# A two-layer decoder trunk on one core: ScalarE reads the last tile from PSUM, the last root lies in PSUM, and GpSimd adds three blocks to the residual

## The chip, the cores and the metric

The kernel runs on one core of one Trainium2 chip. The metric is the device time of one execution in microseconds (us), as a median over runs. Beside the timed runs there is one execution taken by the hardware profiler; it gives the rows shown here.

## The reference

Two layers are applied to 512 prompt tokens and 8 decode tokens that share one set of weights. Cut to what matters here:

```
h = x + RMSNorm_post ( Mixer ( RMSNorm_pre (x) ) )
y = h + RMSNorm_post2( SwiGLU( RMSNorm_pre2(h) ) )

RMSNorm(f, w) = f * rsqrt(mean(f*f) + eps) * w          # over the 1024 features of a token
SwiGLU(h)     = (silu(h @ Wgate) * (h @ Wup)) @ Wdown    # 22 blocks of 128 hidden features
```

Mixer is a gated DeltaNet group and a retention group between an input and an output projection; the change doesn't touch it. The change is in the last line of the last layer: the down projection gives f, the sum of squares over its features gives the root, and f, weighted by w and multiplied by the root, is added to the residual h.

## The kernel before, in words

**Layout.** Activations lie transposed: features on the 128 partitions in KT = 8 blocks, tokens in the free dimension. The 520 tokens are split in two halves `a` = 0 and 1 of HC = 260 columns each. `hT[:, k, a]` is block k of the residual in half a, `fT[:, k, a]` the same block of the sublayer's output; both are fp32 in SBUF. One block of one half is 128 x 260 x 4 bytes = 133,120 bytes.

**The down projection.** TensorE makes the eight output blocks one after the other. Each is a sum over 22 hidden blocks, with three matmuls per hidden block and half (values are split in a high and a low part). Blocks 0 to 6 are done for both halves together. The last block, k = 7, is made half by half: all 66 matmuls of half 0 into PSUM bank 2 (semaphore `half_done`), then those of half 1 into bank 3 (`tile_done`). The matmuls that add up squares over the partitions (`sum_added` at L692, `norm_sum` at L698) are put into that second run: after hidden block 0 and hidden block 2 of half 1 for half 0; after the last one for half 1. They write banks 4 and 5.

**The norm.** For each block, VectorE copies PSUM to `fT`, ScalarE squares it into `sqb` (`square`, L1333) and then weights `fT` in place by the norm's weight (`weigh`, L1382). `root_mean` is two ScalarE instructions: Ln from PSUM (L1344) and Exp (L1345), which leave the root in `rb[:, a]` in SBUF. `new_h` is run by VectorE for a group of blocks k0 to k1: it multiplies `fT` by the root (L1908), waits for that, and adds the product to `hT` (L1909). Each semaphore wait stands in the in-order queue of its engine: what is behind it waits too.

**The end of the last layer.** VectorE copies block 7 of half 0 (L2577), runs `new_h` for half 0 in the groups (0,1), (1,2), (2,3), (3,4), (4,6), (6,8), and, between the last two of them, copies block 7 of half 1 from PSUM (L2589). Then it runs `new_h` for half 1 in the three groups of `LAST`. SyncE sends five parts of `hT` to `yT` (L566), each when `h_ready` has reached its last block; the last three parts are the groups of `LAST`:

```
LAST = [(0, 4), (4, 7), (7, 8)]
Y_PARTS = [(0, 0, 4), (0, 4, 8)] + [(1, k0, k1) for k0, k1 in LAST]
```

**GpSimd** has other work earlier in the kernel (decay factors, some products, and the loads and stores of the decode states); nothing of it is in the last stage after its last store.

Of the kernel before, what the change touches and what calls it, by code (L numbers as in the profile page):

```python
# [8 lines left out]
def trunk(nc, xT, w_slabs, w_ba, w_rows, dt_bias, a_log, conv_hist, state_gdn, state_ret, c_f32, c_rope,  # L9
# [4 lines left out]
    ALU = mybir.AluOpType  # L14
    ACT = mybir.ActivationFunctionType

    P = 128
# [82 lines left out]
    with ctx:  # L100
# [285 lines left out]
        def heads_of(i):  # L386
# [1 line left out]
            return i // 2, slice((i % 2) * P, (i % 2 + 1) * P)  # L388

        names = (  # L390
            "const_loaded mask_loaded row_loaded early_loaded adt_loaded rope_reloaded x0_loaded x1_loaded x2_loaded "
            "x3_loaded x4_loaded first_loaded slab0_loaded slab1_loaded dst0_loaded dst1_loaded dst0_stored dst1_stored tail_stored "
            "state_stored y_stored a_stored a_loaded xq_stored x_loaded "

# [78 lines left out]
        block = ctx.enter_context(nc.Block())  # L473


        LAST = [(0, 4), (4, 7), (7, 8)]
        Y_PARTS = [(0, 0, 4), (0, 4, 8)] + [(1, k0, k1) for k0, k1 in LAST]

        @block.sync
        def _(sp):  # L480
# [37 lines left out]
            sp.dma_start(cf[:], c_f32).then_inc(s["const_loaded"], 16)  # L518
            sp.dma_start(wba[:], w_ba).then_inc(s["early_loaded"], 16)
            sp.dma_start(rope[:], c_rope).then_inc(s["early_loaded"], 16)  # L520
            sp.dma_start(mask[:], c_mask).then_inc(s["mask_loaded"], 16)
            sp.dma_start(histT[:], conv_hist).then_inc(s["early_loaded"], 16)
            for l in range(DEPTH):
                for n in range(SLABS):
# [49 lines left out]
        def _(pool):  # L574
# [13 lines left out]
            for l in range(DEPTH):  # L588
                def read_state(u):
                    if u < 2:  # L590

                        for a in range(2):
                            pool.wait_ge(s[f"tile_free{a}"], l * TILES // 2 + 4)
                    else:
                        pool.wait_ge(s["dr_mm"], l * 16 + u - 1)
                    load_state(l, u, True)

                def masked_step(i):
                    if i == 0:
                        pool.wait_ge(s["mask_loaded"], 16)  # L600
                        pool.wait_ge(s["xq_stored"], (l + 1) * 32)
                    mk = mask[:, 0:1, :].unsqueeze(1).to_broadcast([P, 2, 2, P])
                    to = T[:, i].rearrange("p (c a) n -> p c a n", c=2)
                    nc.gpsimd.tensor_tensor(to, MT[:, 2 * i:2 * i + 2, 2:4], mk, ALU.mult).then_inc(s["mtk_ready"], 1)

                def keys_decayed(c):
                    if c == 0:
                        pool.wait_ge(s["mt_ready"], (l + 1) * NC)
                        pool.wait_ge(s["kt_ready"], (l + 1) * NC)
                    nc.gpsimd.tensor_tensor(ktok[:, c], ktok[:, c], over_cols(c2[:, c, :]), ALU.mult).then_inc(s["kd_ready"], 1)  # L610

                def decay_rests(c):
                    if c >= 2:
                        pool.wait_ge(s["dec_mm"], l * NC + c - 1)
                    else:
                        pool.wait_ge(s["g_split"], l + 1)
                        pool.wait_ge(s["rod_mm"], (l + 1) * NC)
                        pool.wait_ge(s["state_stored"], l * 32)
                    nc.gpsimd.tensor_tensor(dinl[c % 2], over_heads(m_le), over_cols(g2[:, 1, c].bitcast(fp32)), ALU.mult).then_inc(s["dkl_ready"], 1)

                for u in range(8):
                    read_state(u)
                for c in range(NC):
                    decay_rests(c)
                for u in range(8, 10):
                    read_state(u)
                for c in range(NC):

                    pool.wait_ge(s["a_ready"], l * NC + c + 1)
                    nc.gpsimd.tensor_tensor(MT[:, c, 2:4], MT[:, c, 2:4], Ab[:, 0:2, c], ALU.add).then_inc(s["cm_ready"], 1)  # L630
                pool.wait_ge(s["aT_T"], (l + 1) * NC)
                nc.gpsimd.memset(kqpad, 0.0).then_inc(s["x_zeroed"], 1)
                pool.wait_ge(s["cm_ready"], (l + 1) * NC)
                pool.wait_ge(s["a_stored"], (l + 1) * NBK * 16)
                nc.gpsimd.memset(Xc[:].rearrange("p i h c n -> p (i h c n)"), 0.0).then_inc(s["x_zeroed"], 1)
                pool.wait_ge(s["tO_T"], (l + 1) * NC)
                nc.gpsimd.memset(XT[:].rearrange("p c h n -> p (c h n)"), 0.0).then_inc(s["x_zeroed"], 1)
                masked_step(0)
                masked_step(1)
                for u in range(10, 16):  # L640
                    read_state(u)
                for c in range(NC):
                    keys_decayed(c)
                for c in range(1, NC):
                    pool.wait_ge(s["qs_mm"], l * (NC - 1) + c)
                    pool.wait_ge(s["s_ready"], l * NC + c)
                    nc.gpsimd.tensor_tensor(S[:], S[:], over_cols(egc[:, 1, c, :]), ALU.mult).then_inc(s["s_decayed"], 1)
                pool.wait_ge(s["dr_mm"], (l + 1) * 16)
                pool.wait_ge(s["w_rest"], l * REST + (Q - 1) * W_STEPS + W_LO05)
                load_state(l, 0, False)  # L650
                load_state(l, 1, False)
                for u in range(16):
                    store_state(l, u)
                    if u < 14:
                        pool.wait_ge(s[f"dst{u % 2}_stored"], 16 * (l * 8 + u // 2 + 1))
                        load_state(l, u + 2, False)
                if l + 1 < DEPTH:
                    for a in range(2):
                        pool.wait_ge(s[f"dst{a}_stored"], 16 * (l + 1) * 8)
                    pool.dma_start(rope[:], c_rope).then_inc(s["rope_reloaded"], 16)  # L660

        @block.tensor
        def _(pe):
# [624 lines left out]
        def _(act):  # L1288
# [16 lines left out]
            for l in range(DEPTH):  # L1305
# [26 lines left out]
                    to = sqh[:, k % 2] if a is None else sqh[:, k % 2, a]  # L1332
                    A(to, src, ACT.Square).then_inc(s["sq_ready" if n % 2 else "xsq_ready"], 2 if a is None else 1)  # L1333

                def root_mean(n, a, l=l):
                    T0 = l * TILES
                    if n % 2 == 0:
                        act.wait_ge(s["x_sums"], nth_norm(l, n) + nth(l, n, KT - 1, a))
                    else:
                        act.wait_ge(s["norm_sum"], (l * 2 + n // 2) * 2 + a + 1)  # L1340

                        for u in range(2):
                            act.wait_ge(s[f"tile_free{u}"], (T0 + (32 if n == 1 else T_DN)) // 2)
                    step(A(rb[:, a], PS[:, 4 + a, 0:HC], ACT.Ln, scale=1.0 / D, bias=EPS))  # L1344
                    A(rb[:, a], rb[:, a], ACT.Exp, scale=-0.5).then_inc(s["rb_ready"], 1)  # L1345

                def round_x(n, k, a, l=l):

# [142 lines left out]
                for t in range(32):  # L1491
# [4 lines left out]
                    if t == 6:  # L1496
                        act.wait_ge(s["gate_pre"], l + 1)
                        if l == 0:
                            act.wait_ge(s["adt_loaded"], DEPTH * 32)
                        A(gb[:], ga[:, :, 0:H], ACT.Exp, scale=-1.0)  # L1500
                        A(adt[:, l, 1, :], adt[:, l, 1, :], ACT.Exp)
                        step(A(gs[:], gs[:], ACT.Exp, scale=-1.0))
# [309 lines left out]
                def square_down(k):  # L1812
# [3 lines left out]
                    else:  # L1816
                        square(3, k, fT[:, k, 1], 1)

                for i in range(KT * FT // 8 - NW):
                    hi(G0 + S_DN + i + NW)  # L1820
                    for k in range(KT - 2):
# [3 lines left out]
                                weigh(3, k - 1, fT[:, k - 1])  # L1825
                weigh(3, KT - 3, fT[:, KT - 3])
                square_down(KT - 2)
                act.wait_ge(s["half_free"], (l + 1) * SPLIT)
                square(3, KT - 1, fT[:, KT - 1, 0], 0)
                weigh(3, KT - 2, fT[:, KT - 2])  # L1830
                weigh(3, KT - 1, fT[:, KT - 1, 0], 0)
                if l + 1 < DEPTH:
                    root_mean(3, 0)
                    hi(G0 + SLABS)
# [17 lines left out]
                    second_x(0, l + 1)  # L1852
                else:
                    root_mean(3, 0)
                    square_down(KT - 1)
                    weigh(3, KT - 1, fT[:, KT - 1, 1], 1)
                    root_mean(3, 1)

        @block.vector
        def _(dve):  # L1860
# [12 lines left out]
            for l in range(DEPTH):  # L1873
# [201 lines left out]
                for t in range(32):  # L2075
# [39 lines left out]
                    if t == 5:  # L2115
# [2 lines left out]
                        step.go(V.tensor_copy(places, flat2(rD[:, 0:H]).rearrange("p (u j) -> p j u", j=4)))  # L2118
                        dve.wait_ge(s["bad_done"], l + 1)
                        if l == 0:  # L2120
                            dve.wait_ge(s["adt_loaded"], DEPTH * 32)
                        step.go(V.tensor_copy(ga[:, 0:NC, :].rearrange("p c h -> p (c h)"), PS[:, 7, B_BA:B_BA + NC * 2 * H]))
                        step(V.tensor_copy(ga[:, NC:NG, :].rearrange("p c h -> p (c h)"), PS[:, 6, 0:NB * 2 * H]))
                        step(V.tensor_tensor(ga[:, :, H:2 * H], ga[:, :, H:2 * H], adt[:, l, 0, :].unsqueeze(1).to_broadcast([P, NG, H]), ALU.add))
# [448 lines left out]
                    if 3 <= i < 19:  # L2573
                        new_state(i - 3)
                down_tile(KT - 2)
                dve.wait_ge(s["half_done"], (l + 1) * SPLIT)
                V.tensor_copy(fT[:, KT - 1, 0], PS[:, 2, 0:HC]).then_inc(s["half_free"], 1)  # L2577
                dve.wait_ge(s["half_free"], (l + 1) * SPLIT)
                for k0, k1 in (*TOGETHER[:2], (2, 3), (3, 4), *TOGETHER[3:]):
                    new_h(3, k0, k1, 0)  # L2580
                    if k0 == 0:
# [1 line left out]
                    for k in range(max(k0 - 1, 0), k1 - 1 if l + 1 < DEPTH else 0):  # L2583
                        rest_x(0, k, 0, l + 1)
                        if k == 1:
                            lo(G0 + SLABS + 1)
                    if k0 == (2 if l + 1 < DEPTH else 4):
                        done(T_DN + KT - 1)
                        freed(V.tensor_copy(fT[:, KT - 1, 1], PS[:, 3, 0:HC]), T_DN + KT - 1)  # L2589
                if l + 1 < DEPTH:  # L2590
                    rest_x(0, KT - 1, 0, l + 1)
                evacuated(T_DN + KT - 1)
                if l + 1 < DEPTH:
                    second_half_x(3, l + 1)
                    lo(G0 + SLABS + 2)
                else:
                    for k0, k1 in LAST:
                        new_h(3, k0, k1, 1)


def _constants(nc_, heads, seq, nb, past_len=4096, rope_base=10000.0):
# [120 lines left out]
```

## Time and profile before

| what | value |
|---|---|
| time, median of 3 runs | 1384.03 us |
| lowest and highest of these | 1383.95 and 1384.6 us |
| the profiled execution's own time | 1382.82 us |
| its span (first to last recorded instruction) | 1381.0 us |
| granted TensorE clock, mean | 0.997 |
| busy share: TensorE, VectorE, ScalarE, GpSimd | 99%, 75%, 46%, 7% |
| HBM read and written | 132.79 and 12.78 MB |

The span is 1.82 us shorter than the profiled execution's own time; that rest lies around the recorded instructions. Times within the trace count from the start of the span. A row of a timeline shows when an instruction starts and how long it takes; in square brackets stands how long its engine had been idle and what released it. In the chain that ended last, each piece is what the next one waited for.

### The profile page before, as it was taken

To read this page: it belongs to the slowest core of one execution; us is meant where nothing else is said; L and a number is where in the kernel's file an instruction comes from. 1 tells how busy PE (TensorE), PEld (TensorE's weight loads), DVE (VectorE), ACT (ScalarE), POOL (GpSimd) and SP (SyncE) were. 2 spreads that over 40 slices of the span, in tenths; PEclk is the share of its full clock that TensorE was granted. 3 is DMA by queue.
4 is the path that set the end of the run, shared out by engine and by line. 5 is a ranking of instruction groups with operands and counts; after the bars stand their busy time and mean duration, and the time that the engine had idled before them with its cause. 6 is when DMAs were issued, how large, how long until landed. Compare 5 with 4: busy or idle time off the path is not lost.

```text
span 1381.0 us, 29088 instructions
## 1 busy us (share of the span) xinstructions
PE 1361.7 (99%) x12172; PEld 1339.7 (97%) x12172; DVE 1039.5 (75%) x1675; ACT 634.9 (46%) x1230; POOL 100.6 (7%) x141
## 2 busy tenths in 40 slices
PE   9999999999999999999999999999999999999997
PEld 8999999999999999999989999999999999999996
DVE  7746896867998898754586558958789989886545
ACT  5235554557544455422442364545575445454221
POOL 0001211000000000011000012110000000000110
PEclk9999999999999999999999999999999999999998
DMA  5322233122323232345413313321222323233542
GB/s 210 112 103 77 73 116 113 32 68 92 104 98 117 96 111 104 121 164 182 131 62 112 115 55 95 108 94 40 75 92 93 123 92 114 101 108 123 174 177 93
DMA packets 67491, 147.46 MB, mean 107 GB/s; under 512 B 20128, under 2 KB 23584, under 8 KB 67360
## 3 DMA queue, kind: packets, MB, share of 16 engines
q1 hardware_dynamic: 59248, 119.37, 25.9%
q0 software_dynamic: 7824, 25.70, 5.3%
q8 instruction: 96, 1.57, 0.5%
q10 hardware_dynamic: 288, 0.52, 0.1%
q14 instruction: 35, 0.29, 0.1%
HBM read 132.79 MB, written 12.78 MB: 105 GB/s over the span
## 4 chain that ended last, share of the span: by engine, by line
PE 88%; DVE 8%; ACT 1%; issue 1%; DMA 1%; SPq 0%; DVEq 0%; ACTq 0%
PE PS L669 48%; PE PS L1224 8%; PE PS L1225 8%; PE PS L1226 8%; PE PS L675 5%; DVE Wl L1871 1%; DVE hT L1909 1%; DVE Xl L1888 1%; DVE mT L1908 1%; PE PS L863 1%; DVE conv L1998 1%; PE PS L1190 1%; PE PS L847 1%; PE PS L835 1%; PE PS L1009 1%
## 5 line engine op out<-in xcount | busy, mean ns | idle before, releaser
L1303 ACT ACTIVATE Wh<-stage 128x1024 fp32r<-128x1024 f32 x143 | 151.1, 1058 | 327.2 <-PE PS L669 300.1
L669 PE MATMUL PS<-Xh,Wh 128*128 128x260 f32 x1376 | 285.3, 288 | 2.3 <-DVE Wl L1933 1.6
L669 PE MATMUL PS<-Xh,Wl 128*128 128x260 f32 x1376 | 277.0, 283 | 0.0
L669 PE MATMUL PS<-Xl,Wh 128*128 128x260 f32 x1376 | 276.5, 282 | 0.0
L1871 DVE TENSOR_TENSOR Wl<-stage,Wh 128x1024 fp32r<-128x1024 f32 x143 | 174.6, 1222 | 105.4 <-ACT Wh L1303 104.6
L669 PEld LDWEIGHTS PS<-Xh,Wh 128*128 128x128 f32 x1376 | 211.4, 189 | 5.6 <-DVE Wl L1933 2.0
L669 PEld LDWEIGHTS PS<-Xh,Wl 128*128 128x128 f32 x1376 | 211.8, 188 | 0.0
L669 PEld LDWEIGHTS PS<-Xl,Wh 128*128 128x128 f32 x1376 | 211.7, 188 | 0.0
L1224 PE MATMUL PS<-XU,hiA 128*128 128x260 f32 x448 | 126.8, 283 | 0.0
L1224 PE MATMUL PS<-XU,hiB 128*128 128x260 f32 x448 | 126.8, 283 | 0.0
L1225 PE MATMUL PS<-XU,hiB 128*128 128x260 f32 x448 | 126.6, 283 | 0.0
L1225 PE MATMUL PS<-XU,hiA 128*128 128x260 f32 x448 | 126.6, 283 | 0.0
L1226 PE MATMUL PS<-XU,loB 128*128 128x260 f32 x448 | 126.4, 282 | 0.0
L1226 PE MATMUL PS<-XU,loA 128*128 128x260 f32 x448 | 126.4, 282 | 0.0
L669 PE MATMUL PS<-actH,Wh 128*128 128x260 f32 x616 | 124.1, 282 | 0.0
L669 PE MATMUL PS<-actH,Wl 128*128 128x260 f32 x616 | 123.9, 282 | 0.0
L669 PE MATMUL PS<-actL,Wh 128*128 128x260 f32 x616 | 123.9, 282 | 0.0
L669 PEld LDWEIGHTS PS<-actH,Wh 128*128 128x128 f32 x616 | 97.2, 188 | 1.4
L669 PEld LDWEIGHTS PS<-actL,Wh 128*128 128x128 f32 x616 | 94.8, 188 | 0.0
L669 PEld LDWEIGHTS PS<-actH,Wl 128*128 128x128 f32 x616 | 94.8, 188 | 0.0
L1225 PEld LDWEIGHTS PS<-XU,hiA 128*128 128x128 f32 x448 | 84.7, 189 | 0.0
L1225 PEld LDWEIGHTS PS<-XU,hiB 128*128 128x128 f32 x448 | 84.7, 189 | 0.0
(384 smaller groups left out, 2865.7 us busy)
## 6 DMA issues: line engine op xcount, KB each, us to landing
stage<-w_slabs SPq DMA_DIRECT2D x143, 512.0 KB, 3.3
raw<-w_slabs SPq DMA_DIRECT2D x136, 256.0 KB, 2.7
dst<-state_ret POOLq DMA_DIRECT2D x32, 256.0 KB, 3.3
dst<-state_gdn POOLq DMA_DIRECT2D x32, 256.0 KB, 3.9
out_gdn_sample<-dst POOLq DMA_DIRECT2D x16, 256.0 KB, 2.9
out_ret_sample<-dst POOLq DMA_DIRECT2D x16, 256.0 KB, 3.2
hT<-x_t SPq DMA_DIRECT2D x3, 520.0 KB, 6.5
out_y_t<-hT SPq DMA_DIRECT2D x3, 520.0 KB, 3.1
```

The costliest lines, as they stand in the source:

```text
L669: ins = mm(pj(slot)[:, a], w[:, ws, pos, :], x[:, a, :], start=first and w is Wh and x is xh, stop=last and w is Wl)
L675: ins = mm(pj(slot)[:, a], w[:, ws, pos, :], x[:, a, :], start=first and w is Wh and x is xh, stop=last and w is Wl)
L835: ins = mm(PS[:, 6, h * P:(h + 1) * P], rT[:, H + h, cs], rT[:, h, cs], start=True, stop=True)
L847: ins = mm(PS[:, 4, h * P:(h + 1) * P], T[:, 0, h, :], T[:, 1, h, :], start=True, stop=True)
L863: ins = mm(PS[rows, 7, B_U:B_U + P], vectors, dst[:, u % 2, j, :], start=n == 0, stop=n == 7 and u < 8, skip_group_check=True)
L1009: ins = mm(PS[:, 4 + c, h * P:(h + 1) * P], kT[:, h, cs], qT[:, h, cs], start=True, stop=True)
L1190: mm(PS[:, 4 + u % 2, :], krows[:, u // 8, :], vblks[u % 2].rearrange("p a n -> p (a n)"), start=True, stop=True).then_inc(s["outer_mm"], 1)
L1224: mm(PS[:, bank, 0:HC], hi_[:, u, cols], XU[:, u, 0, k], start=k == 0 and u in (UA11, US2, US1, UA22), stop=False, skip_group_check=True)
L1225: mm(PS[:, bank, 0:HC], hi_[:, u, cols], XU[:, u, 1, k], start=False, stop=False, skip_group_check=True)
L1226: ins = mm(PS[:, bank, 0:HC], lo_[:, u, cols], XU[:, u, 0, k], start=False, stop=k == 3, skip_group_check=True)
L1303: A(Wh[:, G % NW], stage[:, G % NS], ACT.Copy).then_inc(s["hi_split"], 1)
L1871: V.tensor_tensor(Wl[:, G % NW], stage[:, G % NS], Wh[:, G % NW].bitcast(fp32), ALU.subtract).then_inc(s["lo_split"], 1)
```

## The change

In the last layer only:

- VectorE's two copies of block 7 out of PSUM are gone. A new ScalarE helper, `last_half(a)`, squares the block straight from PSUM and writes the weighted block from PSUM to `fT`. The weighting of block 6 now stands ahead of it.
- The Exp that ends `root_mean` for half 1 writes to PSUM bank 6 instead of `rb[:, 1]`.
- Half 1's residual: VectorE multiplies blocks 0 to 2 by the root, then blocks 3 to 7 (`f_scaled` counts both). GpSimd waits for the first, adds blocks 0 to 2 to `hT`, and raises `h_ready` by 3. VectorE waits for its own two products and for GpSimd's add (by `h_ready`), and then adds blocks 3 to 6 and block 7.
- `LAST` is (0,3), (3,7), (7,8), so the last three stores have other sizes.
- The mask's load near the kernel's start counts on `adt_loaded` instead of a semaphore of its own, whose place `f_scaled` takes; the three waits on `adt_loaded` and the one on the mask wait for all five loads.

```
-        LAST = [(0, 4), (4, 7), (7, 8)]
+        LAST = [(0, 3), (3, 7), (7, 8)]
 ...
-            sp.dma_start(mask[:], c_mask).then_inc(s["mask_loaded"], 16)
+            sp.dma_start(mask[:], c_mask).then_inc(s["adt_loaded"], 16)
 ...
-                        pool.wait_ge(s["mask_loaded"], 16)
+                        pool.wait_ge(s["adt_loaded"], (2 * DEPTH + 1) * 16)
 ...
+            k1 = LAST[0][1]
+            pool.wait_ge(s["f_scaled"], 1)
+            nc.gpsimd.tensor_tensor(hT[:, 0:k1, 1], hT[:, 0:k1, 1], fT[:, 0:k1, 1], ALU.add).then_inc(s["h_ready"], k1)
 ...
-                    A(rb[:, a], rb[:, a], ACT.Exp, scale=-0.5).then_inc(s["rb_ready"], 1)
+                    A(rb[:, a] if root is None else root, rb[:, a], ACT.Exp, scale=-0.5).then_inc(s["rb_ready"], 1)
 ...
+                def last_half(a):
+
+                    if a:
+                        act.wait_ge(s["tile_done"], T0 + TILES)
+                    else:
+                        act.wait_ge(s["half_done"], (l + 1) * SPLIT)
+                    square(3, KT - 1, PS[:, 2 + a, 0:HC], a)
+                    row = R_FPOST + KT - 1
+                    A(fT[:, KT - 1, a], PS[:, 2 + a, 0:HC], ACT.Copy, scale=prm[:, l, row:row + 1]).then_inc(s["f_ready"], 1)
 ...
+                if l + 1 == DEPTH:
+                    weigh(3, KT - 2, fT[:, KT - 2])
+                    last_half(0)
+                else:
                     (the four lines of before)
 ...
                     root_mean(3, 0)
-                    square_down(KT - 1)
-                    weigh(3, KT - 1, fT[:, KT - 1, 1], 1)
-                    root_mean(3, 1)
+                    last_half(1)
+                    root_mean(3, 1, root=PS[:, 6, 0:HC])
 ...
-                    if k0 == (2 if l + 1 < DEPTH else 4):
+                    if k0 == 2 and l + 1 < DEPTH:
                         done(T_DN + KT - 1)
                         freed(V.tensor_copy(fT[:, KT - 1, 1], PS[:, 3, 0:HC]), T_DN + KT - 1)
 ...
-                    for k0, k1 in LAST:
-                        new_h(3, k0, k1, 1)
+                    dve.wait_ge(s["rb_ready"], (l * 4 + 4) * 2)
+                    dve.wait_ge(s["f_ready"], (l + 1) * HN)
+                    for k0, k1 in (LAST[0], (LAST[1][0], KT)):
+                        src = fT[:, k0:k1, 1]
+                        V.tensor_tensor(src, src, PS[:, 6:7, 0:HC].to_broadcast([P, k1 - k0, HC]), ALU.mult).then_inc(s["f_scaled"], 1)
+                    dve.wait_ge(s["f_scaled"], 2)
+                    dve.wait_ge(s["h_ready"], nth_norm(l, 3) + KT + LAST[0][1])
+                    for k0, k1 in LAST[1:]:
+                        V.tensor_tensor(hT[:, k0:k1, 1], hT[:, k0:k1, 1], fT[:, k0:k1, 1], ALU.add).then_inc(s["h_ready"], k1 - k0)
```

## Rows read from the trace of the kernel before

**Rows 1.** The page: span, and the shares of the chain that ended last.

```profile
span 1381.0 us, 29088 instructions
...
PE 88%; DVE 8%; ACT 1%; issue 1%; DMA 1%; SPq 0%; DVEq 0%; ACTq 0%
```

**Rows 2.** Chain that ended last, 1369 to 1381 us: start, length (us), what.

```profile
1368.92 1.09 PE PS L675 x9
...
1370.10 0.44 DVE fT L2589
...
1370.56 0.43 ACT sqb L1333
...
1371.04 0.72 PE PS L698 x2
...
1371.78 0.40 ACT rb L1344
...
1372.20 0.43 ACT rb L1345
...
1372.82 1.25 DVE fT L1908
...
1374.16 1.25 DVE hT L1909
...
1375.44 0.98 DVE fT L1908
...
1376.52 0.98 DVE hT L1909
...
1377.52 0.44 DVE fT L1908
...
1377.98 0.43 DVE hT L1909
```

**Rows 3.** Timeline of half 0's norm and around the last copy: start, us, instruction.

```profile
1361.78 0.42 ACT L1333 ACTIVATE sqb<-fT 128x260 f32<-128x260 f32 x1 [5.76 <-DVE fT L2577]
...
1362.57 0.38 PE L698 MATMUL PS<-sqb,cf 128*128 128x260 f32 x1
...
1369.83 0.60 PE L692 MATMUL PS<-ss,cf 128*128 128x260 f32 x2
...
1371.02 0.51 ACT L1382 ACTIVATE fT<-fT,prm 128x260 f32<-128x260 f32 x1
...
1371.24 0.70 DVE L1909 TENSOR_TENSOR hT<-hT,fT 128x520 f32<-128x520 f32 x1
```

**Rows 4.** Quarter-microsecond windows: busy times, then TensorE clock, DMA share, GB/s.

```profile
1376.25:1376.50 0.25, 0.00 (x0) 0.00 (x0) 0.16 (x1) 0.00 (x0) 0.00 (x0) 0.50 0.53 187
...
1377.75:1378.00 0.25, 0.00 (x0) 0.00 (x0) 0.22 (x2) 0.00 (x0) 0.00 (x0) 0.50 0.53 175
...
1378.25:1378.50 0.25, 0.00 (x0) 0.00 (x0) 0.17 (x1) 0.00 (x0) 0.00 (x0) 0.50 0.19 71
...
1379.75:1380.00 0.25, 0.00 (x0) 0.00 (x0) 0.00 (x0) 0.00 (x0) 0.00 (x0) 0.50 0.81 283
```

**Rows 5.** Groups by line and shape: ScalarE's squares of 260 columns from PSUM.

```profile
L1743 ACT ACTIVATE sqb<-PS 128x260 f32<-128x260 f32 x34 | 12.6, 370 | 0.2
```

**Rows 6.** Timelines of GpSimd and VectorE where both work: 151 to 153, 222 to 227 us.

```profile
152.02 0.73 POOL L630 TENSOR_TENSOR MT<-MT,Ab 128x256 f32<-128x256 f32 x1 [3.52 <-DVE Ab L2025]
...
151.25 0.68 DVE L2025 TENSOR_TENSOR Ab<-PS,brk 128x512 f32<-128x512 f32 x1
...
222.41 4.03 POOL L610 TENSOR_TENSOR ktok<-ktok,c 128x512 f32<-128x512 f32 x4
...
222.53 0.69 DVE L2051 TENSOR_TENSOR T<-PS,brkm 128x512 f32<-128x512 f32 x1 [1.86 <-PE PS L956]
223.14 3.36 DVE L2171 TENSOR_TENSOR sqd<-qkvD 128x32 f32<-128x32 f32 x1
226.42 0.18 DVE L2172 TENSOR_TENSOR sqd<-qkvD 128x32 f32<-128x32 f32 x1
```

**Rows 7.** One line's instructions: count, shortest, median and longest in ns.

```profile
L604 POOL TENSOR_TENSOR T<-MT,mask x4: 1347/1648/1777, 198.4 to 885.3; 128x512 f32<-128x512 f32 x4
```

More of the change, by code:

```diff
@@ L390, in trunk @@
         names = (
-            "const_loaded mask_loaded row_loaded early_loaded adt_loaded rope_reloaded x0_loaded x1_loaded x2_loaded "
+            "const_loaded f_scaled row_loaded early_loaded adt_loaded rope_reloaded x0_loaded x1_loaded x2_loaded "
             "x3_loaded x4_loaded first_loaded slab0_loaded slab1_loaded dst0_loaded dst1_loaded dst0_stored dst1_stored tail_stored "
@@ L1333, in square, with root_mean @@
                     A(to, src, ACT.Square).then_inc(s["sq_ready" if n % 2 else "xsq_ready"], 2 if a is None else 1)
-                def root_mean(n, a, l=l):
+                def root_mean(n, a, l=l, root=None):
                     T0 = l * TILES
@@ L1498, in _ @@
                         if l == 0:
-                            act.wait_ge(s["adt_loaded"], DEPTH * 32)
+                            act.wait_ge(s["adt_loaded"], (2 * DEPTH + 1) * 16)
                         A(gb[:], ga[:, :, 0:H], ACT.Exp, scale=-1.0)
@@ L1827, in _ @@
                 square_down(KT - 2)
[L1828 to L1831, printed above, removed]
+                if l + 1 == DEPTH:
+                    weigh(3, KT - 2, fT[:, KT - 2])
+                    last_half(0)
+                else:
+                    act.wait_ge(s["half_free"], (l + 1) * SPLIT)
+                    square(3, KT - 1, fT[:, KT - 1, 0], 0)
+                    weigh(3, KT - 2, fT[:, KT - 2])
+                    weigh(3, KT - 1, fT[:, KT - 1, 0], 0)
                 if l + 1 < DEPTH:
@@ L2120, in _ @@
                         if l == 0:
-                            dve.wait_ge(s["adt_loaded"], DEPTH * 32)
+                            dve.wait_ge(s["adt_loaded"], (2 * DEPTH + 1) * 16)
                         step.go(V.tensor_copy(ga[:, 0:NC, :].rearrange("p c h -> p (c h)"), PS[:, 7, B_BA:B_BA + NC * 2 * H]))
@@ L2575, in _ @@
                 down_tile(KT - 2)
-                dve.wait_ge(s["half_done"], (l + 1) * SPLIT)
-                V.tensor_copy(fT[:, KT - 1, 0], PS[:, 2, 0:HC]).then_inc(s["half_free"], 1)
-                dve.wait_ge(s["half_free"], (l + 1) * SPLIT)
+                if l + 1 < DEPTH:
+                    dve.wait_ge(s["half_done"], (l + 1) * SPLIT)
+                    V.tensor_copy(fT[:, KT - 1, 0], PS[:, 2, 0:HC]).then_inc(s["half_free"], 1)
+                    dve.wait_ge(s["half_free"], (l + 1) * SPLIT)
                 for k0, k1 in (*TOGETHER[:2], (2, 3), (3, 4), *TOGETHER[3:]):
@@ L2591, in _ @@
                     rest_x(0, KT - 1, 0, l + 1)
-                evacuated(T_DN + KT - 1)
+                    evacuated(T_DN + KT - 1)
                 if l + 1 < DEPTH:
```

## The prediction

> **What bounds the kernel now.** I read the page first. TensorE carries 88% of the chain that ended last and VectorE 8% [rows 1]. The edits to the computation lie after or beside the last matmuls of layer 2, so what they are worth is read there, not from the shares. Next the same chain, narrowed to the last microseconds [rows 2]. The reader is to see one serial tail. The last matmul ends at 1368.92 + 1.09 = 1370.01. Then come the copy of block 7 (VectorE), its square (ScalarE), the sum over partitions (TensorE), Ln and Exp (ScalarE), and from 1372.82 six VectorE instructions, a product and a sum for each group of `LAST`, to 1378.41. Nothing overlaps in it.
>
> Third, the timeline around it, for what lies beside the chain [rows 3], and last the stores in windows of a quarter microsecond [rows 4]. The DMA engines are busy in two solid stretches. The first begins about 1376.37 (0.53 of the window that ends at 1376.50) and ends at 1377.88: 1.51 us for the four blocks that were ready at 1375.40. The second begins at 1378.45 and ends at 1379.95, 1.50 us for the three blocks ready at 1377.50 and the one ready at 1378.41. So a store's bytes begin to move 0.97 us after the sum (1376.37 - 1375.40; 0.95 in the other case), and a block takes 1.51 / 4 = 0.38 us (133,120 bytes at some 350 GB/s). The last block alone could have begun at 1378.41 + 0.97 = 1379.38, but the three ahead of it are through only at 1378.45 + 3 x 0.38 = 1379.59. The end is therefore set by the store of the second group, not by the last sum: already before, the last block queues for 0.2 us.
>
> **The change part by part.**
>
> *The start.* The mask's load changes its semaphore. All five loads lie in the first stage, and the first reader of the mask runs near 198 us [rows 7]. Nothing is added; cost 0. Were a load late after all, GpSimd, VectorE and ScalarE would each wait in order behind it, but 100 us and more of other work covers it.
>
> *Half 0.* Without the copy, the square can start about 0.45 us before 1361.78. But its sum stands in TensorE's queue after hidden block 2 of half 1, at 1362.57, behind a square that had ended at 1362.20 [rows 3]. TensorE did not wait for it, so worth 0; its cover is 0.37 us. Moving the weighting of block 6 ahead costs nothing, because ScalarE had been idle 5.76 us there [rows 3]. VectorE, which no longer copies block 7 of half 1, finishes half 0 near 1370.85 instead of 1371.94 [rows 3]; it then waits for the root anyway. Worth 0 too.
>
> *Block 7 of half 1 from PSUM.* The copy goes. Before, 0.55 us passed from the matmul's end to the square (1370.01 to 1370.56, [rows 2]); a wake-up of 0.07 remains, so ScalarE starts at 1370.08. The square from PSUM costs 0.37 [rows 5] against 0.42: TensorE's sum starts at 1370.08 + 0.43 = 1370.51. TensorE is free then: its first part of the sum starts 1369.83, lasts 0.60 and ends at 1370.43 [rows 3]. That is a cover of only 0.08 us. With 0.72 for the sum and 0.02 to ScalarE, Ln starts at 1371.25, Exp 0.42 later at 1371.67, and VectorE 0.62 after that, all steps as in [rows 2]: 1372.29 instead of 1372.82. Gain 0.53. The weighting, 0.51 before [rows 3], runs beside the sum in either kernel. Where Exp writes is priced as before: no row has an Exp into PSUM. Above, I bound it by the present 0.42; below, by a read of PSUM, 0.37, so 0.05 either way.
>
> *Products.* A VectorE operation of 260, 780, 1040 columns takes 0.43, 0.98, 1.25 (chain, [rows 2]): 0.27 per block on 0.16. The product over three blocks ends at 1372.29 + 0.98 = 1373.27. That over five costs 0.16 + 5 x 0.27 = 1.51 and ends at about 1374.80. Its PSUM operand should not make it dearer: 512 columns with one operand in PSUM took 0.69 [rows 6], where this scale gives 0.16 + 512/260 x 0.27 = 0.69.
>
> *GpSimd's sum.* It starts 0.09 us after VectorE's signal (151.25 + 0.68 = 151.93 to 152.02, [rows 6]), at 1373.36. No row has 780 columns. The nearest, two full fp32 operands of 256 columns, is 0.73 [rows 6]. In proportion that gives 0.73 x 780/256 = 2.22, the upper bound if GpSimd has any fixed cost. The lower comes from 4.03/4 = 1.01 per 512 columns with a small second operand [rows 6]: 1.54. The dearest row, 1.78 for 512 columns of bf16 mask beside VectorE work [rows 7], gives 2.71 and stays as an outer bound. I take 2.0, near the first row, less a small fixed part. GpSimd ends at 1375.36. VectorE, finished at 1374.80, waits for it; both remaining sums and both last stores are queued behind that wait. With 0.1 to wake it (my estimate, as in the other direction), it adds four blocks from 1375.46 to 1376.70 and block 7 to 1377.16. Before: 1378.41. So the arithmetic ends 1.25 us sooner.
>
> The case turns on whether the product and GpSimd's sum run together. At 222.41 four GpSimd operations fill 4.03 us. A VectorE operation with one PSUM operand started at 222.53 and took its usual 0.69; the next, both operands from SBUF and only 32 columns, took 3.36, until GpSimd was through, against 0.18 for its like [rows 6]. The products now read the root from PSUM, so they are of the first kind; the sums are of the second, but they start after GpSimd. The Trainium skill says the same (SBUF — State Buffer, "Who interferes with whom": a VectorE instruction with at most one SBUF input, outside the two-port modes, does not contend with GpSimd, one with two does against a GpSimd read); the trace agrees, 0.69 against 3.36. A second rule speaks against the change: the Trainium skill (GPSIMD Engine Reference, "Elementwise — side-by-side cycle accounting") gives 4497 ns on GpSimd for a 2048-column fp32 add against 2293 on VectorE. In proportion, an estimate of 1.71 us for 780 columns: slower than VectorE's 0.98, yet shorter than my 2.0, and by it the gain would be 0.3 more.
>
> *Stores.* Here most of the 1.25 goes. GpSimd's three blocks: bytes from 1375.36 + 0.97 = 1376.33 to 1377.46. The four blocks ready at 1376.70: from 1377.67 for 1.51 to 1379.18. The last, ready at 1377.16, could flow at 1378.13 but queues until 1379.18 and ends at 1379.56, against 1379.95. The last store now queues for one microsecond, since its predecessor has four blocks instead of three.
>
> *Sum.* 0.39, say 0.4 us less: on the profiled execution 1382.82 (span 1381.0 and 1.82 around it) becomes 1382.4, and on the median, which is 1.21 higher, 1384.03 becomes 1383.6.
>
> **The rivals.**
> - *All of the arithmetic's gain reaches the end.* If stores overlap rather than queue, the end follows the last sum: 1384.03 - 1.25 = 1382.8. A GpSimd sum of 1.5 us comes near it: then the four-block sum starts at 1375.0, gain 0.9. Against it: four blocks took the same 1.5 us as one store or as two [rows 4].
> - *GpSimd is dearer than thought (slower than before).* Each 0.1 us of its sum moves the four-block store by 0.1. Break-even is 2.0 + 0.4 = 2.4 us; with 2.71 [rows 7] the kernel ends 0.3 later: 1384.3. For it: the row exists. Against: that row had VectorE operations on two SBUF operands beside it, and another type.
> - *The two engines exclude each other after all.* GpSimd starts after the second product, at 1374.89, and ends at 1376.89; four blocks are summed by 1378.23, and bytes end at 1378.23 + 0.97 + 1.89 = 1381.09, 1.14 later: 1385.2. The 0.69 in [rows 6] speaks against it.
> - *Something elsewhere moves*, by a shifted instruction stream in the 1370 us that are unchanged. Nothing in the profile speaks for it.
>
> **How the numbers follow.** A measurement of this kernel can tell about 0.2% from no change, 2.8 us, twice what the whole tail could give. Chances: forecast (gain 0.1 to 0.8, 1383.2 to 1383.9) 0.55; all of the gain or near it, 0.18; dear GpSimd 0.15; exclusion 0.05; something elsewhere 0.07, of which 0.03 beyond 0.2% faster and 0.02 slower. The first four all lie within 0.2%, so same is 0.95. The range takes in the first rival (1382.8) and the second (1384.3), each with 0.3 for the scatter that the three runs show: 1382.5 to 1384.6.
>
> **What the profile after should show.** The square of block 7 starts 0.1 us after the last matmul. VectorE's first product of half 1 starts 2.3 us after it instead of 2.8. GpSimd's one operation lasts about 2.0 us, beside an undisturbed 1.5 us product. VectorE idles some 0.7 us, released by GpSimd, then two sums. DMA is busy without a gap for 1.9 us at the end, starting about 1.0 us after the four-block sum. The prediction would be wrong if the five-block product is stretched, if GpSimd takes over 2.4 us, or if a span outside the last 11 us moves.

## The result: 0.18% slower, and the profile after

The changed kernel takes 1386.15 us (median of 21 runs, 1384.53 to 1389.37) against 1383.95 us for the kernel before (21 runs, 1382.14 to 1385.27): ratio 1.0018, 95% interval [1.0012, 1.0024]. The forecast was 1383.6 us, within 1382.5 to 1384.6; it missed on the slow side by 2.55 us. The ratio lies just under the 0.2% that the prediction gave as the least that can be told, but the interval does not hold 1: by it the change costs 1.7 to 3.3 us.

I count a **tail** from the end of half 1's last matmul to the end of the span, since the point where the tail begins moves by itself: it lay between 1369.8 and 1372.5 in the fourteen profiled executions of this case, with no order by kernel. Two things in the part that the change leaves alone go with it. In six traces (the changed kernel, three variants of it and two of the kernel before) TensorE pauses for 1.1 to 1.3 us near 208 us, waiting for ScalarE's `bv`, and the last matmul ends at 1371.5 to 1372.5. In three others the granted TensorE clock was 0.83 instead of 1.00 between 5 and 15 us, and it ends at 1371.1 to 1371.5. The five with neither end at 1369.8 to 1370.8. Why an execution has the one or the other was not tried. Before, the tail is 1381.0 - 1370.01 = 10.99 us. In the changed kernel the span is 1385.8 and the last matmul ends at 1372.16, so the tail is 13.64: 2.65 longer. The chain that ended last in the changed kernel (start, length, what):

```profile
1367.97 4.19 PE PS L678 x35
1372.16 0.44 PE PS L695 x2
1372.60 0.04 issue
1372.64 0.72 PE PS L701 x2
...
1373.38 0.40 ACT rb L1347
...
1373.80 0.40 ACT PS L1348
...
1374.23 0.41 issue
1374.65 0.98 DVE fT L2618
...
1375.73 1.87 POOLq L100
...
1377.72 1.24 DVE hT L2622
1378.97 0.34 DVEq L100
```

and its groups of instructions in the last 14 us (x count, busy us, mean ns, idle before and its releaser):

```profile
L663 POOL TENSOR_TENSOR hT<-hT,fT 128x780 f32<-128x780 f32 x1 | 1.8, 1829 | 18.1 <-DVE fT L2618 18.1
L2618 DVE TENSOR_TENSOR fT<-fT,PS 128x1300 f32<-128x1300 f32 x1 | 1.5, 1501 | 0.0
L2622 DVE TENSOR_TENSOR hT<-hT,fT 128x1040 f32<-128x1040 f32 x1 | 1.2, 1242 | 0.7 <-POOL hT L663 0.7
...
L1336 ACT ACTIVATE sqb<-PS 128x260 f32<-128x260 f32 x1 | 0.4, 387 | 6.0 <-PE PS L678 6.0
```

The chain names the GpSimd sum by L100, since the exit's instruction already stands in GpSimd's queue, and it stops at VectorE's last sum: stores and exit are not in it. Up to there the end of the work is as forecast, though not each step. VectorE's first product starts 2.49 us after the last matmul (forecast 2.28, before 2.81). GpSimd's sum took 1.83 us, VectorE waited 0.7 us for it, and the last sum ended at 1377.72 + 1.58 = 1379.30. That is 7.14 us after the last matmul; forecast 7.15, before 8.40. The stores, in the same quarter-microsecond windows as [rows 4]:

```profile
1378.50:1378.75 0.25, 0.00 (x0) 0.00 (x0) 0.25 (x1) 0.00 (x0) 0.00 (x0) 0.50 0.82 287
...
1379.75:1380.00 0.25, 0.00 (x0) 0.00 (x0) 0.00 (x0) 0.00 (x0) 0.00 (x0) 0.50 0.23 83
...
1381.75:1382.00 0.25, 0.00 (x0) 0.00 (x0) 0.00 (x0) 0.00 (x0) 0.00 (x0) 0.50 0.35 113
1382.00:1382.25 0.25, 0.00 (x0) 0.00 (x0) 0.00 (x0) 0.00 (x0) 0.00 (x0) 0.50 0.00 0
```

The last byte moves at 1381.84, 9.68 us after the last matmul, against 9.94 before. But then nothing is busy for 3.96 us, where 1.05 passed before (1379.95 to 1381.0). The instructions of the program's exit say why (all have one line; op, duration ns, first and last start). First the changed kernel, then the kernel before:

```profile
L100 POOLq EVENT_SEMAPHORE  x2: 17/17/17, 1385.7 to 1385.7; - x2
...
L100 POOLq DRAIN  x1: 9876/9876/9876, 1375.7 to 1375.7; - x1
...
L100 SPq DRAIN  x1: 7/7/7, 1382.6 to 1382.6; - x1
...
L100 SPq EVENT_SEMAPHORE  x1: 17/17/17, 1385.8 to 1385.8; - x1
```

```profile
L100 POOLq DRAIN  x1: 8564/8564/8564, 1355.0 to 1355.0; - x1
...
L100 SPq DRAIN  x1: 7/7/7, 1380.8 to 1380.8; - x1
```

Every engine ends with a drain, and then they meet. SyncE is through at 1382.6 and waits for GpSimd. GpSimd's drain stands in its queue from 1375.73 and takes 9.88 us: 1.87 us of it is the sum itself (the chain's piece), 8.01 us comes after the sum. The drain is not new. In the kernel before it follows GpSimd's last store at 1355.0 and takes 8.56 us, of which some 0.55 is that issue: 8.0 us again, but over at 1363.5, and nobody notices.

### The profile page after: what moved, and what is told of

Same layout as the page of the kernel before. It is cut to its first block, busy times and chain, and to the rows that moved or that the text cites. A ratio compares the mean times of both kernels' runs of the same rounds, so it can differ in the third digit from the quotient of the medians.

```text
span 1385.8 us, 29080 instructions
## 1 busy us (share of the span) xinstructions
PE 1362.8 (98%) x12172; PEld 1340.0 (97%) x12172; DVE 1039.4 (75%) x1671; ACT 634.6 (46%) x1230; POOL 103.0 (7%) x142
## 4 chain that ended last, share of the span: by engine, by line
PE 87%; DVE 8%; ACT 1%; issue 1%; DMA 1%; SPq 0%; POOLq 0%; DVEq 0%; ACTq 0%
PE PS L672 48%; PE PS L1227 8%; PE PS L1228 8%; PE PS L1229 8%; PE PS L678 5%; DVE Wl L1887 1%; DVE hT L1925 1%; DVE Xl L1904 1%; DVE mT L1924 1%; PE PS L866 1%; DVE conv L2014 1%; PE PS L1193 1%; PE PS L850 1%; PE PS L838 1%; PE PS L1012 1%
```

## The experiments

All runs stand beside runs of the kernel before on the same chip. "The drain beyond its instruction" is the closing GpSimd drain less the part in which its last instruction still runs.

### VectorE does GpSimd's sum

```
-            pool.wait_ge(s["f_scaled"], 1)
-            nc.gpsimd.tensor_tensor(hT[:, 0:k1, 1], ..., ALU.add)
...
-                    dve.wait_ge(s["h_ready"], nth_norm(l, 3) + KT + LAST[0][1])
-                    for k0, k1 in LAST[1:]:
+                    for k0, k1 in LAST:
```

> The changed kernel without its GpSimd sum: VectorE adds blocks 0 to 2 itself, then 3 to 6 and 7; all else as changed. I count the tail from the end of half 1's last matmul to the span's end: 10.99 us before (1370.01 to 1381.0), 13.64 after (1372.16 to 1385.8). Theory (closing drain): in the changed kernel GpSimd's drain ends about 8.0 us after its last instruction, and the program waits for it. Without that instruction the drain starts after GpSimd's last store, near 1357, and is hidden: the tail is set by the stores again, about 2.49 to the first product + 2.4 for two products + 0.1 + 2.5 for three sums = 7.5, stores done at about 10.0, end at 11.0; time 1384.0, as before. Rival A (the loss is in the new store sizes or in the longer wait of the last store): the sizes are the same, so the tail stays above 13 and the time near 1386.2. Rival B (something earlier in the program was shifted by the new semaphore use): unchanged here too, 1386 or so, with a last matmul near 1372.

Measured 1384.1 us (11 runs; before 1383.75; ratio 1.0002 [0.9993, 1.001]). The last matmul ended at 1371.42 and the span at 1382.5, a tail of 11.1. GpSimd's exit:

```profile
L100 POOLq DRAIN  x1: 8564/8564/8564, 1356.4 to 1356.4; - x1
```

The loss is gone with the one GpSimd instruction and the wait for it, though the sizes of the stores, the PSUM reads and the semaphores are those of the changed kernel. Rivals A and B fall.

### The PSUM reads alone

```
-                    square_down(KT - 1)
-                    weigh(3, KT - 1, fT[:, KT - 1, 1], 1)
+                    last_half(1)
                     root_mean(3, 1)
```
(and the same for half 0; `LAST` and `new_h` as before, root in SBUF)

> The kernel before with one part of the change alone (and the mask's semaphore as changed): ScalarE squares and weights block 7 from PSUM, VectorE's two copies are gone. The root stays in SBUF, the three groups are (0,4), (4,7), (7,8), VectorE does all sums. By my prediction's own term for this part the tail shrinks by 0.53 from 10.99 to 10.5 and the time is 1383.5. Rival A: reading PSUM from ScalarE twice costs what the copy did, tail 11.0, time 1384.0. Rival B (something earlier is shifted by the mask's new semaphore): 1385.5 with a tail of 10.5.

1383.69 us (11 runs; before 1383.75; ratio 0.9998 [0.9989, 1.0007]); last matmul 1370.00, span 1380.7, tail 10.70. The chain:

```profile
1370.47 0.72 PE PS L698 x2
...
1371.63 0.43 ACT rb L1345
1372.06 0.04 DVEq L1918
1372.10 0.41 issue
1372.51 1.25 DVE fT L1921
```

The sum over partitions starts 0.57 us earlier than in [rows 2]; TensorE is no obstacle. But between Exp and the first product 0.45 us pass instead of 0.20, so 0.30 of the forecast 0.53 remains. All ten profiled kernels without VectorE's copy have the pause of about 0.4 before this product, whether Exp writes to SBUF or PSUM; the four with the copy have not. It isn't a matter of a long wait alone: in half 0 of the kernel before, VectorE had waited 2.39 us and started 0.09 after Exp. Its cause wasn't tried.

### A fill that nobody waits for, at three times

The kernel before, with one more GpSimd instruction; the three differ in its wait:

```
+            pool.wait_ge(s["h_ready"], DEPTH * 2 * HN - 4)
+            nc.gpsimd.memset(gs[:], 0.0)
```

After half 1's first sum:

> The kernel before with one more GpSimd instruction: a fill of 48 columns of a buffer that nobody reads any more, after VectorE's first sum of half 1. Nobody waits for it. Theory (closing drain of 8.0 us after GpSimd's last instruction, and the program ends only after it): VectorE's first sum ends 5.39 us after the last matmul, so 5.39 + 0.1 + 0.1 + 8.0 + 0.2 = 13.8 instead of 10.99, and the time is 1384.0 + 2.8 = 1386.8. Rival (the changed kernel lost because of what its GpSimd sum does or what waits for it, or by stores): nothing waits here and nothing is stored, so 1384.0 and a tail of 11.0.

After the last sum (`DEPTH * 2 * HN`):

> As the one before, but the fill comes after VectorE's last sum, which ends 8.40 us after the last matmul. Theory (closing drain): 8.40 + 0.1 + 0.1 + 8.0 + 0.2 = 16.8, time 1384.0 + 5.8 = 1389.8; the two fills differ by just the 3.0 us between the two sums. Rival: 1384.0 again. If the drain waited for something else, such as stores or the other engines, the two fills would end at the same time.

After half 0's root (`rb_ready`, `DEPTH * 8 - 1`):

> The kernel before with the same 48-column GpSimd fill, but after half 0's root, which comes 5.97 us before the last matmul (1364.04 against 1370.01). Theory (8.0 us closing drain): the drain ends at -5.97 + 0.1 + 0.1 + 8.0 = 2.3 us after the last matmul, long before the stores: tail 11.0, time 1383.9, as before. Rival (any late GpSimd instruction costs its 2 to 3 us, wherever it stands in the last stage): 1386.

| fill after | expected time, tail | median (runs), ratio | tail |
|---|---|---|---|
| half 0's root | 1383.9, 11.0 | 1383.77 (10), 1.0 [0.9991, 1.0009] | 11.0 |
| first sum | 1386.8, 13.8 | 1386.17 (10), 1.0016 [1.0007, 1.0025] | 13.8 |
| last sum | 1389.8, 16.8 | 1390.44 (4), 1.0046 [1.0031, 1.0061] | 16.8 |

For the fill after the last sum, its instruction and GpSimd's and SyncE's exit:

```profile
1380.93 0.14 POOL L662 MEMSET gs<- 128x48 f32 x1 [22.94 <-DVE hT L1911]
```

```profile
L100 POOLq DRAIN  x1: 8151/8151/8151, 1380.9 to 1380.9; - x1
...
L100 SPq DRAIN  x1: 7/7/7, 1383.2 to 1383.2; - x1
```

A fill of 0.14 us that touches nothing still in use costs almost 6 us at the end, and nothing 14 us earlier. So neither the sum's own price nor who waits for it is the cause; what counts is when GpSimd's last instruction ends.

### The root in SBUF

```
-                    root_mean(3, 1, root=PS[:, 6, 0:HC])
+                    root_mean(3, 1)
...
-                        V.tensor_tensor(src, src, PS[:, 6:7, 0:HC].to_broadcast(...), ALU.mult)
+                        V.tensor_tensor(src, src, rb[:, 1:2].to_broadcast(...), ALU.mult)
```

> The changed kernel with the root in SBUF instead of PSUM; GpSimd still adds three blocks. If a VectorE product with both operands in SBUF and a GpSimd sum exclude each other, GpSimd's instruction waits for the five-block product or the other way round: it ends some 1.4 us later than the 5.4 us after the last matmul of the changed kernel, and as the drain is counted from it, the tail is 13.64 + 1.4 = 15.0 and the time 1387.5. If they do not exclude each other: tail 13.7 and 1386.2.

1388.67 us (5 runs; before 1383.79; ratio 1.0031 [1.0018, 1.0044]); last matmul 1372.52, span 1387.4, tail 14.9. GpSimd's sum and VectorE's five-block product:

```profile
1376.15 2.96 POOL L663 TENSOR_TENSOR hT<-hT,fT 128x780 f32<-128x780 f32 x1 [18.10 <-DVE fT L2618]
```

```profile
L2618 DVE TENSOR_TENSOR fT<-fT,rb 128x1300 f32<-128x1300 f32 x1 | 1.5, 1507 | 0.0
```

The sum takes 2.96 instead of 1.83, the product keeps its 1.5. GpSimd, which came second, is the one held up. The exclusion that [rows 6] show is real, and the root in PSUM avoids it.

### An explicit drain ahead of GpSimd's wait

```
+            nc.gpsimd.drain()
             pool.wait_ge(s["f_scaled"], 1)
```

> The changed kernel with an explicit drain of GpSimd ahead of its wait for the first product, where it is idle for 18 us. Theory (every drain takes 8.0 us after the last instruction): the explicit one takes 8 us in hidden time, the closing one takes 8 us again after the sum: 1386.2, tail 13.6. Rival (the 8.0 us are a settling of GpSimd's earlier transfers and work, which need be done only once): the closing drain is short, the end is set by the stores at about 10.7, tail 10.7, time 1383.3.

1383.36 us (10 runs; before 1383.79; ratio 1.0001 [0.9991, 1.0011]); last matmul 1370.08, span 1380.8, tail 10.7. The explicit drain and the closing one:

```profile
L662 POOLq DRAIN  x1: 8562/8562/8562, 1355.0 to 1355.0; - x1
```

```profile
L100 POOLq DRAIN  x1: 1931/1931/1931, 1373.6 to 1373.6; - x1
...
L100 SPq DRAIN  x1: 7/7/7, 1380.6 to 1380.6; - x1
```

Here my theory fell in the form I had given it. The 8 us are not a toll on every drain: once paid, only 0.06 us is left beyond the sum (1.931 - 1.87). That leaves two readings, the first drain of a program, or a settling of something that GpSimd has done since the last one.

### What the drain settles

The changed kernel with one explicit drain at four other places.

As GpSimd's first instruction:

> The changed kernel with an explicit GpSimd drain as its very first instruction, ahead of all its work and its 97 DMA issues; none at the end. The last set showed that a drain after GpSimd's last store takes the 8.0 us off the closing one (0.06 left after the sum). Theory 1 (the cost is of the first drain of a program): the one at the start takes it, the closing drain is short, tail 10.7 (last matmul to end of span), time 1383.4. Theory 2 (a drain settles the transfers that GpSimd issued since the last drain): the closing drain still takes 8.0 us after the sum, tail 13.6, time 1386.2.

Ahead of its last store issue:

> The changed kernel with an explicit drain just before GpSimd's very last store issue: one DMA issue follows it, 20 us before the sum, all others precede it. Theory 1 (first drain of the program): closing drain short, tail 10.7, 1383.4. Theory 2: one issue follows, so the closing drain costs again; 8.0 us if the cost is fixed (tail 13.6, 1386.2), a hundredth of it, and so not to be seen, if it grows with the number of issues (tail 10.7). If theory 1 fails in the other run of this set, this one tells fixed from proportional.

Between the layers:

> The changed kernel with an explicit drain after GpSimd's part of layer 1; 48 of its 97 DMA issues follow it. So far: closing drain beyond the last instruction 8.0 us with 97 issues since the last drain, 0.06 with none, 0.15 with one. Theory (proportional, (8.0 - 0.06) / 97 = 0.082 us each): 0.06 + 48 x 0.082 = 4.0 us after the sum, the explicit one 0.06 + 49 x 0.082 = 4.1 us; the tail is then set by the stores, 10.7. Rival (the cost has a ceiling, or is full from a few issues on): 8.0 us again in both, tail 13.6.

With 14 issues left:

> The changed kernel with an explicit drain after GpSimd's last but 14 DMA issues. Theory (proportional): the closing drain takes 0.06 + 14 x 0.082 = 1.2 us after the sum, the explicit one 0.06 + 83 x 0.082 = 6.9 us; tail 10.7. Rival (ceiling): 8.0 or another value common to 14 and 48 issues.

| drain placed | DMA issues after it | closing drain, us | less the sum's 1.87 or 1.88 | tail |
|---|---|---|---|---|
| nowhere (changed kernel) | 97 | 9.876 | 8.01 | 13.6 |
| at the start | 97 | 9.876 | 8.01 | 13.6 |
| between the layers | 48 | 5.864 | 3.98 | 10.7 |
| with 14 left | 14 | 3.079 | 1.21 | 10.7 |
| before the last store | 1 | 2.021 | 0.15 | 10.8 |
| after the last store | 0 | 1.931 | 0.06 | 10.7 |

The one at the start takes 41 ns itself, and that kernel 1387.01 us (9 runs; ratio 1.0023 [1.0014, 1.0033]), so it isn't the first drain of a program that is dear. The traces said so already: in each of the fourteen, GpSimd has a drain of 0.18 us within the first half microsecond. The one before the last store: 1383.4 us (10 runs; 0.9998 [0.9989, 1.0007]). The two of 48 and 14 have a single time each, 1383.27 and 1384.98 beside 1383.28 of before; their drains are what they were made for:

```profile
L100 POOLq DRAIN  x1: 5864/5864/5864, 1374.3 to 1374.3; - x1
```

```profile
L100 POOLq DRAIN  x1: 3079/3079/3079, 1376.0 to 1376.0; - x1
```

All six lie on a line, 0.06 + 0.082 us for each DMA that GpSimd issued since its last drain, though the transfers themselves had landed long before: the last one at about 1359.5 in the changed kernel, 18 us before the sum ended. Time since the last drain does not explain it: some 52 us with 14 issues left 1.21 us, where 695 us with 48 issues left 3.98. Nor does GpSimd's other work, since only loads and stores lie between the drain and the sum with 14 left. Whether an issue, a byte or a packet is what counts, these runs can't tell: 96 of the 97 transfers move the same 256 KB, one 520 KB. The explicit drains agree where 83 and 96 issues precede them: 7.41 and 8.48 us, less 0.54 of the issue under way, are 6.87 and 7.94, where the line gives 6.87 and 7.93. The one between the layers does not: 5.75 - 0.54 = 5.2 for 49 issues, where the line gives 4.1. It was not the landing of the load issued just before it, which came about 2.0 us before this drain ended (673.6 + 3.7 = 677.3 against 673.6 + 5.7 = 679.3). What held it 1.1 us longer, in the middle of the kernel's work, stays open.

### Smaller groups, with the drain out of the way

```
-        LAST = [(0, 3), (3, 7), (7, 8)]
+        LAST = [(0, 2), (2, 4), (4, 6), (6, 8)]
```

> The changed kernel with the explicit drain ahead of GpSimd's wait (as in the last set, tail 10.72) and other groups: GpSimd adds blocks 0 and 1 only, VectorE multiplies 2 and then 6 blocks and adds (2,4), (4,6), (6,8), each stored on its own. Counted from the first product: products end at 0.70 and 2.5; GpSimd's sum runs from 0.8 to 2.1 and no longer holds VectorE up; sums end at 3.2, 3.8, 4.4; stores flow one behind the other from 3.2 + 0.97 = 4.2 for 6 x 0.38 = 2.3 us and end at 6.5, against 7.2 in the kernel with the drain alone. Tail 10.0, time 1382.8 to 1383.0. Rival (each more store costs its own issue and latency on SyncE's queue, 0.35 to 0.40 us each, and the last two queue there): no gain, tail 10.7, 1383.5.

1383.24 us (11 runs; before 1383.73; ratio 0.9997 [0.9988, 1.0006]); last matmul 1372.50, span 1382.4, tail 9.9 (forecast 10.0), the shortest of all. Its last groups:

```profile
L2623 DVE TENSOR_TENSOR hT<-hT,fT 128x520 f32<-128x520 f32 x3 | 1.9, 696 | 0.1
L2619 DVE TENSOR_TENSOR fT<-fT,PS 128x1560 f32<-128x1560 f32 x1 | 1.8, 1770 | 0.0
L664 POOL TENSOR_TENSOR hT<-hT,fT 128x520 f32<-128x520 f32 x1 | 1.3, 1282 | 17.8 <-DVE fT L2619 17.8
```

GpSimd's sum now fits beside the product, and VectorE no longer waits for it. The tail is 1.1 us shorter than before; the timed runs can't tell so little from no change. How much of it the smaller groups would give without GpSimd was not tried.

## Why the prediction was wrong

- **The step that failed** is the sum's last one, in "Stores" and "Sum": I took the end as the last store plus a constant, and placed GpSimd's instruction as if its cost were its duration and who waits for it. I had read what stands behind the last instruction of VectorE and SyncE, not what stands behind GpSimd's. The drain was in the trace of before, 8.56 us long, hidden by 17 us of other work. The change moved it to after the sum, where it ends at 5.44 + 8.01 + 0.2 = 13.65 us after the last matmul: the measured tail of 13.64. Shown by the fills (the tail follows the time of an unused instruction), by the sum given to VectorE (tail 11.1), and by the explicit drain (10.7, where the forecast gain of 0.4 would have made 10.6). None of the signs that the prediction named could have caught it: the product was not stretched, GpSimd's sum stayed under 2.4 us, the last matmul came 2.15 us later but no later than in the kernel before with a fill (1371.1 to 1372.5), and none of them looked behind the last store.
- **The PSUM reads** were right in mechanism and mis-sized: 0.30 instead of 0.53 (tail 10.70 against 10.99). The square was as priced (0.39 against 0.37), Exp into PSUM 0.39, within its bounds; the missing 0.23 is the pause ahead of the product, 0.45 instead of 0.20. With the drain out of the way the whole change has the same tail of 10.7 as this part alone, so with its groups of blocks the sum on GpSimd gained nothing that the profiles show.
- **GpSimd's sum** took 1.83 where I took 2.0, within 1.54 to 2.22. This error and the first product, 0.21 late, cancelled: that the arithmetic ended at 7.14 against 7.15 was luck. The rule of the Trainium skill (GPSIMD Engine Reference, "Elementwise — side-by-side cycle accounting") gave an estimate of 1.71; the same sum on VectorE took 0.97, a ratio of 1.9 where the page has 1.96.
- **The exclusion** did not occur, which is what was forecast, and it does when the root lies in SBUF (2.96 against 1.83 us); the rule of the Trainium skill (SBUF — State Buffer, "Who interferes with whom") holds here on both sides.
- **The queue of stores** was right: a store's bytes began 0.95 and 0.98 us after the sums, one stretch of 1.90 us at the end, the last byte 9.68 us after the last matmul against 9.55 forecast. Of the 1.26 us that the arithmetic gained, 0.26 reached the stores.
- **The semaphores at the start and half 0** cost nothing that the runs can tell: the kernels that share them are level with the kernel before, within some 1.2 us.

So 0.26 us was won and 2.9 lost to a drain, which makes the tail 2.65 longer; the medians differ by 2.2, and 2.65 lies within the 1.7 to 3.3 us of the interval.

## What to carry to other kernels

Before work is given to an engine near the end, look at how the engine leaves the program, not only at its instructions: its exit may be long, hidden today, and counted from its last instruction. If GpSimd issues many DMAs and then has a late task, drain it explicitly in an idle stretch ahead of that task, and check that the task is worth it: here, with the groups of the change, the blocks given to GpSimd gained nothing over reading PSUM from ScalarE alone. And when several stores end a kernel, ask which store's bytes end last: a shorter sum helps only as far as the stores ahead of the last one start earlier.

## What the runs showed of the hardware that I had not expected

- GpSimd's drain took 0.06 us plus 0.082 us for each DMA that it had issued since its last drain, long after they had landed: 8.01 us for 97, 3.98 for 48, 1.21 for 14, 0.15 for 1 (all but one of them transfers of 256 KB). One drain in the middle of the kernel took 1.1 us more than that.
- VectorE's first product started 0.45 us after the Exp that it waits for instead of 0.20 wherever its copy of block 7 was gone; not explained.
- The end of the last matmul moved between 1369.8 and 1372.5 us from one profiled execution to another, more than all that the change does to the tail's arithmetic; a TensorE pause of 1.1 to 1.3 us near 208 us or a granted clock of 0.83 between 5 and 15 us went with the later ones. Parts of a tail are to be compared from a common point.
